# A hybrid encoder layer on Trainium2: one stick feature tile ahead in the linear attention, squares for two norms in the tails of the projections ahead of them, and memory queries without a copy

## What is computed

```python
h = h + mix @ w_out                       # mix = gated linear attention (4 heads) | stick-breaking attention (8 heads)
h = h + mem_xattn(rmsnorm(h, g_mem_q), rmsnorm(mem, g_mem_kv))   # 256 memory tokens, 4 heads of 256
h = h + peer(rmsnorm(h, g_ffn))           # 8 heads x 16 experts for each token, gathered from 16384
return rmsnorm(h, g_final)

def rmsnorm(x, g):
    return x * rsqrt(mean(x * x) + EPS) * g

# linear attention, 16 chunks of 64 tokens, a state carried from chunk to chunk
o_inter = (q * exp(b)) @ state
o = o_inter + attn(q, k, decay) @ v
state = state * exp(b_last) + (k * exp(b_last - b)).T @ v
```

## Time and profile before

| what | us |
|---|---|
| median of 3 runs | 3696.14 |
| lowest and highest | 3693.44 and 3697.06 |
| the profiled execution, its own time | 3697.59 |
| its span, first to last instruction | 3695.9 |
| mean granted TensorE clock, share of full speed | 0.918 |

### The profile page before, as it was taken

How to read it: one execution, slowest core, us unless ns; L and a number is a source line. 1 busy time by engine, 2 the same in 40 slices (tenths; PEclk the granted TensorE clock), 3 DMA queues, 4 the chain that set the end, 5 groups by cost and what they waited for, 6 DMA issues and landing times.

```text
span 3695.9 us, 32347 instructions
## 1 busy us (share of the span) xinstructions
PE 2885.4 (78%) x8696; PEld 1455.1 (39%) x8696; DVE 2555.4 (69%) x5661; ACT 1501.0 (41%) x3958; POOL 1537.7 (42%) x1176
## 2 busy tenths in 40 slices
PE   6899999787988688778877888766666666666675
PEld 5777544676833233343323333322222222222221
DVE  3453453534477877888778777877787787778776
ACT  3221596322233543554344433444344334434343
POOL 0000021000045545555445545566656565655555
PEclk9999999898999899889999999998888898888889
DMA  2101002221399999999999999999999999999998
GB/s 80 41 23 46 1 1 102 75 74 59 130 367 418 417 418 416 407 403 419 416 411 414 414 415 412 406 409 418 412 404 420 417 418 413 414 410 417 412 415 348
DMA packets 177613, 1155.95 MB, mean 313 GB/s; under 512 B 19985, under 2 KB 22049, under 8 KB 46241
## 3 DMA queue, kind: packets, MB, share of 16 engines
q0 software_dynamic: 147456, 1073.81, 70.7%
q1 hardware_dynamic: 29984, 80.26, 6.2%
HBM read 1149.80 MB, written 4.19 MB: 312 GB/s over the span
## 4 chain that ended last, share of the span: by engine, by line
DMA 39%; PE 11%; ACT 8%; issue 7%; DVE 5%; POOL 2%; POOLq 0%; DVEq 0%; ACTq 0%
DMA early_rows<-in_uv,choice_index 22%; DMA rows<-in_uv,choice_index 17%; PE expert_acc L2194 10%; ACT L2070 2%; ACT L1360 2%; DVE expert_own_acc L1944 1%; DVE early_rows L1968 1%; ACT expert_wt L2072 1%; POOL early_rows L1460 1%; POOL rows L1460 1%; ACT expert_dg L2081 1%; DVE rows L1968 1%; ACT expert_wt L2070 1%; ACT choice_best L1360 1%; PE expert_side L2120 0%
## 5 line engine op out<-in xcount | busy, mean ns | idle before, releaser
L2194 PE MATMUL expert_acc<-early_rows,expert_dg 128*128 128x512 f32 x1756 | 959.2, 682 | 375.8 <-ACT expert_dg L2081 372.5
L1460 POOL DMA_INDIRECT early_rows<-in_uv,choice_index x586 | 838.2, 1430 | 743.3 <-PE expert_acc L2194 388.3
L2194 PE MATMUL expert_acc<-rows,expert_dg 128*128 128x512 f32 x1316 | 726.3, 686 | 298.2 <-ACT expert_dg L2081 295.0
L1968 DVE CUSTOM_DVE_ANT_0 early_rows<-early_rows,expert_xn 128x1024 f32<-128x1024 f32 x586 | 716.8, 1223 | 321.5 <-DMA early_rows<-in_uv,choice_index 317.9
L1460 POOL DMA_INDIRECT rows<-in_uv,choice_index x438 | 649.9, 1484 | 522.5 <-PE expert_acc L2194 282.3
L2070 ACT ACTIVATE expert_wt<-expert_dot 128x1 f32<-128x1 f32 x1024 | 207.4, 203 | 1482.7 <-DVE expert_dot L1968 1481.8
L2194 PEld LDWEIGHTS expert_acc<-early_rows,expert_dg 128*128 128x128 f32 x1756 | 348.3, 213 | 944.6 <-ACT expert_dg L2081 629.7
L1968 DVE CUSTOM_DVE_ANT_0 rows<-rows,expert_xn 128x1024 f32<-128x1024 f32 x438 | 535.6, 1223 | 232.9 <-DMA rows<-in_uv,choice_index 228.8
L2194 PEld LDWEIGHTS expert_acc<-rows,expert_dg 128*128 128x128 f32 x1316 | 263.1, 214 | 733.1 <-ACT expert_dg L2081 486.1
L2081 ACT ACTIVATE expert_dg<-ident,expert_wt 128x128 f32<-128x128 f32 x768 | 308.4, 402 | 25.2
L2072 ACT ACTIVATE expert_wt<-expert_wt,choice_gate 128x1 f32<-128x1 f32 x1024 | 301.3, 294 | 33.3
(11 more groups left out here) (362 smaller groups left out, 3958.6 us busy)
## 6 DMA issues: line engine op xcount, KB each, us to landing
early_rows<-in_uv,choice_index POOLq DMA_INDIRECT x586
H<-in_x SPq DMA_DIRECT2D x8, 1024.0 KB, 10.1
pq_w_raw<-in_w_pq SPq DMA_DIRECT2D x16, 512.0 KB, 3.5
expert_w_raw<-in_w_pq SPq DMA_DIRECT2D x32, 256.0 KB
rows<-in_uv,choice_index POOLq DMA_INDIRECT x438
stick_w_raw<-in_w_feat SPq DMA_DIRECT2D x8, 512.0 KB, 3.6
tok_w_raw<-in_w_tok SPq DMA_DIRECT2D x8, 512.0 KB, 4.2
out_w_raw<-in_w_out SPq DMA_DIRECT2D x8, 512.0 KB, 6.2
```

What stands on the lines that cost most here:

```text
L1460: pool.indirect_dma_start(out=self.rows[R % self.ROWS], out_offset=None, in_=uv, in_offset=bass.IndirectOffsetOnAxis(ap=index, axis=0), bo ...
L1968: nc.vector.tensor_tensor_reduce(rows[R % ROWS][:, 0:D], rows[R % ROWS][:, 0:D], xn[:, :], 1.0, 0.0, ALU.mult, ALU.add, dot[:, h % 2, r:r ...
L2194: last_mm = nc.tensor.matmul(acc[:, h * HALF:(h + 1) * HALF], dg[:, n % DG, :], rows[R % ROWS][:, D + h * HALF:D + (h + 1) * HALF], start= ...
```

## The change

Three edits.

1. In `gla_phase` PE makes half 0 of tile 0 before it waits for anything of block 0. In block b it then makes half 1 of tile b where half 0 stood, and half 0 of tile b+1 where half 1 stood. The last block has nothing between its chunks. DVE's copy of the first half stands behind `operand` of block 0; all others stay where they were and take the other half. PE's loop is written out.
2. `mixout` and `memout` get `squares`: behind its last weight piece ACT sums the squares of each block of tokens as soon as DVE has added its last part (and of the two memory blocks once they have landed). `norm_phase` gets these sums and skips its own.
3. `memory_attention_phase` loses `mem_qb`: PE reads `q_a` in place. For b >= 2 PE's scores wait for the exponentials of b-2, which read the same bank.

```diff
-def norm_phase(co, name, tok, nb, gain, place, rstd, loads=()):
+def norm_phase(co, name, tok, nb, gain, place, rstd, loads=(), sums=None):
-        ms = co.sb(f"{name}_ms", [P, nb], ctx=cx)
+        ms = sums or co.sb(f"{name}_ms", [P, nb], ctx=cx)
-            for b in range(0, nb, 2):
+            for b in range(0, 0 if sums else nb, 2):
-            for b in range(1, nb, 2):
+            for b in range(1, 0 if sums else nb, 2):
...
+            tok, ms, first, before = squares
+            squared = co.sem(f"{name}_squared")
+            junk = cx.enter_context(nc.psum_tensor(f"{name}_junk", [P, D], F32))
...
             co.high_of_next(act)
+            if squares:
+                link = Chain(act, squared)
+                for b in range(first, nb + before):
+                    if b < before:
+                        act.wait_ge(extra, 16 * len(loads))
+                    else:
+                        act.wait_ge(bank_free, nb * n_chunks + b - before + 1)
+                    link(nc.scalar.activation(junk[:, :], tok(b), ACT.Square, accum_out=ms[:, b:b + 1]))
...
                     w.lows(dve, b, s)
+                if b == 0:
+                    empty(0, 0)
...
-                empty(b, 0)
+                empty(b, 1)
-                    if c:
-                        empty(b, 1)
+                    if c and b + 1 < NB:
+                        empty(b + 1, 0)
...
-            with pe.Fori(0, NB // 2) as i:
+            half(0, 0, 0)
+            for b in range(NB):
...
-                    half(b, s, 0)
+                half(b, s, 1)
...
-                        if c:
-                            half(b, s, 1)
+                    if c and b + 1 < NB:
+                        half(b + 1, 1 - s, 0)
...
-            def queries(b, s):
-                act.wait_ge(s_full, b + 1)
-                nc.scalar.activation(qb[:, s, :, :], q_t[:, :, ds(b * P, P)], ACT.Copy).then_inc(q_ready, 1)
...
-                    queries(b + 2, s)
...
-                pe.wait_ge(q_ready, b + 1)
+                if b >= 2:
+                    pe.wait_ge(probs, MEM_HEADS * (b - 1))
-                        last = nc.tensor.matmul(ps[s][:, h, :], qb[:, s, HD * h + k, :], k_t[:, HD * h + k, :],
+                        last = nc.tensor.matmul(ps[s][:, h, :], q_t[:, HD * h + k, b * P:(b + 1) * P], k_t[:, HD * h + k, :],
...
+            tok_q = lambda b: m_tok[:, b, :] if b < MB else co.H[:, b - MB, :]
+            token_gemm_phase(co, "mixout", by_tokens(x_t), NB // 2, w_out, add, loads=loads + more, squares=(tok_q, sums_q, 0, MB))
...
+                token_gemm_phase(co, "memout", by_tokens(y_t), NB // 2, w_mo, add,
+                                 squares=(lambda b: co.H[:, b, :], sums_f, 0, 0))
```

More of the change, by code:

```diff
@@ L416, in feature_gemm_phase, with token_gemm_phase @@
     co.end_phase()
-def token_gemm_phase(co, name, x, nb, w, evac, loads=()):
+def token_gemm_phase(co, name, x, nb, w, evac, loads=(), squares=None):
     nc = co.nc
@@ L816, in _ @@
             pe.sem_inc(half_full, 2 * HALVES)
-            with pe.Fori(0, NB // 2) as i:
-                for s in range(2):
-                    b = 2 * i + s
-                    wait_alone(co, pe, operands, b + 1)
+            half(0, 0, 0)
+            for b in range(NB):
+                s = b % 2
+                wait_alone(co, pe, operands, b + 1)
+                for h in range(2):
+                    feats = slice(h * CHUNK, (h + 1) * CHUNK)
+                    for a in range(2):
+                        for c in range(NC):
+                            for u in range(NSUB):
+                                last = nc.tensor.matmul(
+                                    pa[h][c * CHUNK:(c + 1) * CHUNK, a, u * SUB:(u + 1) * SUB],
+                                    kh[feats, s, a, c, u, :],
+                                    qh[feats, s, a, c * CHUNK + u * SUB:c * CHUNK + (u + 1) * SUB],
+                                    start=True, stop=True)
+                last.then_inc(scores, 1)
+                for a in range(2):
+                    last = nc.tensor.transpose(pk[:, a * P:(a + 1) * P], kd[:, s, a, :], co.ident[:, :])
+                last.then_inc(turned, 1)
+                half(b, s, 1)
+                pe.wait_ge(masked, b + 1)
+                pe.wait_ge(values, b + 1)
+                pe.wait_ge(o_free, 2 * b + 2)
+                for h in range(2):
+                    for a in range(2):
+                        nc.tensor.matmul(po[h][:, a, :], at[:, s, 2 * a + h, :],
+                                         vb[:, s, (2 * a + h) * GLA_DV:(2 * a + h + 1) * GLA_DV],
+                                         start=(a == 0), stop=False, skip_group_check=True)
+                for c in range(NC):
+                    rows = slice(c * CHUNK, (c + 1) * CHUNK)
+                    if c and b + 1 < NB:
+                        half(b + 1, 1 - s, 0)
+                    wait_alone(co, pe, state_ready, 2 * b + c + 1)
                     for h in range(2):
@@ L832, in _ @@
-                    last.then_inc(scores, 1)
-                    for a in range(2):
-                        last = nc.tensor.transpose(pk[:, a * P:(a + 1) * P], kd[:, s, a, :], co.ident[:, :])
-                    last.then_inc(turned, 1)
-                    half(b, s, 0)
-                    pe.wait_ge(masked, b + 1)
-                    pe.wait_ge(values, b + 1)
-                    pe.wait_ge(o_free, 2 * b + 2)
+                            last = nc.tensor.matmul(po[h][rows, a, :], qi[feats, s, a, rows], state[feats, c, a, :],
+                                                    start=False, stop=(c == NC - 1), skip_group_check=True)
@@ L840, in _ @@
+                    if c == NC - 1:
+                        last.then_inc(o_full, 1)
+                    if c == 0:
+                        wait_alone(co, pe, turned_sb, b + 1)
                     for h in range(2):
+                        feats = slice(h * CHUNK, (h + 1) * CHUNK)
                         for a in range(2):
[L842 to L844 removed]
@@ L868, in gla_phase @@
+                            hd = 2 * a + h
+                            last = nc.tensor.matmul(pst[c][feats, a, :], kt[rows, s, hd * GLA_DK:(hd + 1) * GLA_DK],
+                                                    vb[rows, s, hd * GLA_DV:(hd + 1) * GLA_DV], start=True, stop=True)
+                    last.then_inc(sums, 1)
     co.end_phase()
@@ L1239, in body @@
                 if more:
-                    queries(b + 2, s)
                     exps(b + 2, s)
-            for b in range(2):
-                queries(b, b)
             for b in range(2):
@@ L2296, in program @@
             w_out = pieces("out_w", KT, NB // 2, a['w_out'], mix)
-            token_gemm_phase(co, "mixout", by_tokens(x_t), NB // 2, w_out, add, loads=loads + more)
+            tok_q = lambda b: m_tok[:, b, :] if b < MB else co.H[:, b - MB, :]
+            token_gemm_phase(co, "mixout", by_tokens(x_t), NB // 2, w_out, add, loads=loads + more, squares=(tok_q, sums_q, 0, MB))
         z_b = co.sb("z_b", [P, KT, HALF])
```

44 lines of the change are left out of this document (8 added, 36 removed).

## The result

The changed kernel takes 3675.0 us (median of 5 runs, 3674.4 to 3677.4) against 3696.1 for the kernel before (3693.4 to 3698.1, 5 runs on the same chip): ratio 0.9944, 95% interval 0.9933 to 0.9955, or 21.1 us less. The forecast was 3675.0. The profiled execution took 3675.01 (span 3673.3), 22.6 us less than that of before. That the median meets the forecast to the digit is luck: the interval of the ratio is some 4 us to either side.

What follows compares the result with a forecast made beforehand. The prediction took the last 2670.9 us as bound by transfers, with PE waits in the phases ahead; gains 2.65 + 4.85 + 2.6 + 1.4 + 9.6 = 21.1 us took the median of 3696.1 to 3675.0 us, range 3669 to 3685.

Steps and rivals of the forecast that it cites:

- start of the linear attention: Block 0: half 1 fills PE's 8.09 us wait, PE stays at full clock, values' product starts near 170.2; gain 2.65 us.
- end of the linear attention: Block 7: no half between its chunks, so the last state update starts at about 301.0, not 305.84; gain 4.85 us.
- squares, `memnorms`: Behind `mixout`: ACT squares behind DVE's adds, only the last square is exposed, logarithm at 677.65, not 680.25; gain 2.6 us.
- squares, `ffnnorm`: Behind `memout`: the same with only two squares of each engine saved, logarithm at 900.6, not 901.99; gain 1.4 us.
- memory attention: Queries read in place: block 2's scores follow the turning of block 0 at once, at full clock; gain 9.6 us.
- Middle: Linear attention's steady blocks: the period of 17.94 us and PE's wait for DVE's mask stay; cost 0.
- DVE's variance is made while the table loads: Norm behind `mixout`: variance hidden behind ACT's 1.28 us table load, part of the 2.6 us gain.
- the drain: Norms: about 1380 ns after a table-set switch would keep 1.4 us more each, sum 18.3 us; given no chance of its own.
- the two rivals in which the gathers take time back: Gathering stage: loses 14 us or more, about 3690 (chance 0.06), or runs at a lower rate, slower than before (chance 0.04).
- The rival of the low clock: Linear attention's start and block 2's memory scores: PE stays on low clock, gain 15.8 us, time 3680; chance 0.12.

Runs made afterwards that it cites:

- gla_warm: The kernel before plus a half of unused matmuls in PE's first wait of the linear attention: 3694.2 us against 3695.6, ratio 0.9997.
- written_out: The kernel before with only PE's loop over pairs of blocks in the linear attention written out: 3695.0 us against 3697.3, ratio 0.9994.
- act_copy: The changed kernel with the copy-outs of the halves between the chunks moved from DVE to ACT: 3675.0 us against 3696.3 for the kernel before, ratio 0.9943.
- noload: The changed kernel without the table load in the two norms that get their sums: 3673.8 us against 3696.3 for the kernel before, ratio 0.9939.
- mem_copy_early: The kernel before with all four query copies kept, the third and fourth blocks' moved to where ACT idles: 3685.8 us against 3695.6, ratio 0.9973.
- gla_only: The kernel before with only the first edit, stick features half a tile ahead in the linear attention: 3687.8 us against 3695.7, ratio 0.9980.

## Why the prediction was right, step by step

| step | forecast | measured |
|---|---|---|
| start of the linear attention | 2.65 | 2.92 at block 0, 2.70 left at block 7 |
| end of the linear attention | 4.85 | 4.67 |
| squares, `memnorms` | 2.6 | 2.23 |
| squares, `ffnnorm` | 1.4 | 1.06 |
| memory attention | 9.6 | 10.2 |
| sum, with 2.70 for the start | 21.1 | 20.9 |

The trace's span fell by 22.6 us: 20.9, less 0.4 lost ahead of `mixout` (below), 1.0 and -0.7 between the phases, and 1.8 in the gathering stage. Part of the fit is luck. Memory gave 0.6 us more than forecast and the squares 0.7 less. The start's term held in this trace, and in four of the seven with the same edit it would have been 1.3 us smaller.

**Start.** Right in mechanism, and in size in this trace; `gla_warm` shows the mechanism by itself. The mask ended at 169.85 (row of DVE at 168.60, 1.25 long), not 170.03, and the product followed it.

**Middle.** The period and the wait stayed, as said, in part by luck: written out, the loop gives 0.07 us a block, and the second edit takes 0.07 back. The forecast had both at 0. That a branch's cost lies in PE's wait for the mask is right (`written_out`). The steps of 17.82 us without a branch and 17.95 over one don't show it, though: written out, the first step is the shorter one as well (17.76 and 17.88). One link of the loop was named wrongly: DVE's copy between the chunks isn't in it, as `act_copy` shows. The forecast didn't depend on that link, since nothing of it was changed; my expectation for `act_copy` did, and fell.

**End.** The updates of block 7 are 2.07 us apart where I had 1.9. Of the 7.37 us some 0.4 were lost before `mixout`: ACT's first weights of the next phase are a transfer that didn't move up as far. ACT in `after` from the phase change:

```profile
299.61 1.28 ACT L929 ACT_TABLE_LOAD   x1 [0.92 <-PEq L663]
303.80 1.06 ACT L158 ACTIVATE tok_w_hi<-tok_w_raw 128x1024 fp32r<-128x1024 f32 x1 [2.91 <-DMA tok_w_raw<-in_w_tok]
```

The kernel before waited 2.44 us there. I had not looked at what is late next at this place.

**Squares.** That ACT keeps up with the adds held (0.20 us idle ahead of the last square). What failed is the detail "DVE's variance is made while the table loads": it waits for a signal that ACT sends behind the load, so variance and hand-over stand after it (load ends 670.81, logarithm 671.05, 0.24 where I had 0 and 0.1). The change of phase took 0.44 us to the load and not 0.3. Both together make 0.35 us in each norm. The two norms gave 3.3 us, below the forecast's own bounds of 4.0 with 0.4 on either side.

The Trainium skill (ScalarE: Activation LUTs, What ACT_TABLE_LOAD costs) adds about 1380 ns of drain to a load at every switch to a different set. At the norms this can't be seen: `noload` shows that no set is switched there, and taking the load away gave 1.27 and 1.28 us. The gathering stage does switch, from the set with `Gelu` to that with the exponential and back. ACT in `after`:

```profile
1502.81 0.30 ACT L2079 ACTIVATE expert_wt<-expert_wt,choice_gate 128x1 f32<-128x1 f32 x1
1503.13 1.28 ACT L1367 ACT_TABLE_LOAD   x1
1504.42 0.31 ACT L1367 ACTIVATE choice_best<-choice_best,choice_small 128x16 f32<-128x16 f32 x1
```

From the end of the last activation to the start of the next it is 1.31 us, the load and nothing else. The trace doesn't agree with the drain.

**Memory.** All in the mechanism, and the place of the copies is shown by `mem_copy_early`. The 0.6 us more are rounding in my steps: I took 3.6 us for each group of scores and 1.05 for a turning, their lengths with the overlap; from start to start they are 3.46 and 0.9. The start gave 0.78 and not 1.0. In all eight traces without the late copies the stretch is 37.66 to 37.70 us, so this gain is the same in each.

**The rest.** From the logarithm of `memnorms` to the last copy of `memq` the changed kernel's trace is 1.0 us shorter and from that of `ffnnorm` to the first work of the gathering stage 0.7 longer. Neither belongs to an edit: the stretch from `memk` to `memq` is between 94.2 and 96.0 us long in the traces of all these kernels. The gathering stage was between 2668.2 and 2670.9 us in all of them, at most 2.7 us apart, with up to 31 us saved ahead of it. So the two rivals in which the gathers take time back are refuted here. The rival of the low clock had about the right price: the two kernels with added matmuls show that the clock is worth 3.2 and 2.7 us. In the memory attention it didn't come about in any trace. In the linear attention it stayed away in the changed kernel's trace (granted clock 1.00 behind idle pieces of 1.35 and 0.94 us) and came about in part in four others, where it cost 1.3 us. The forecast that PE stays at full clock there was too sure. The medians can't show these 1.3 us.

## What to carry to other kernels

Before an instruction is removed, look at its place in its engine's list: the same copies of queries cost 9.4 us behind the wrong neighbours and under 1 us in idle time. Where PE idles for some microseconds ahead of dense work, matmuls that are needed anyway, or even ones that are not, can be worth more than their time. Whether the clock stays up behind short idle pieces is to be read from several traces, not from one: kernels with the same edit showed both. For a steady loop write down its links with the releaser of each row, and trust an idle time of 0.34 us: it told that the copy ahead of it was free. The weight piece, with no idle time on either side, was not.

## What the runs showed of the hardware that I had not expected

- A load of a table that is in place already costs its full 1.28 us (`noload`: 1.27 and 1.28 us gained, with no other load taken up), and delays another engine when a signal stands behind it: DVE was idle for 3.00 us ahead of an instruction of 0.17.
- PE's scores of block 0 took 2.43 us behind idle times of 0.91 to 0.95 and 1.16 us, 2.61 behind 1.00 (`gla_only`) and 4.17 behind 8.09; those of one block of the memory attention 3.62 to 3.72 behind at most 2.06, and 6.43 behind 4.07. Idle pieces of 0.9 to 1.4 us don't always leave the clock alone: in four of seven traces it fell to the lower level shortly behind them, for 3 to 4 us (matmuls of 0.63 us among those of 0.39), and in three it didn't.
- Taking PE's four passes out of their loop was worth 0.07 us in every block where PE waits for DVE, with a taken branch ahead of it or without, with no sign of late instructions in the longer code.
- A switch between two table sets cost ACT 1.31 us from one activation to the next, the load alone (row at 1503.13).
